# Gated recurrence of an RWKV-7 branch: the inverse's transposed copy made by 32x32 block transposes on VectorE

## The reference, cut to what matters

```python
def _rwkv7_step(S, inp):
    r, w, k, v, kk, a = inp
    sa = jnp.einsum('dbhij,dbhj->dbhi', S, -kk)
    S = S * w[..., None, :] + sa[..., None] * (kk * a)[..., None, :] + v[..., None] * k[..., None, :]
    y = jnp.einsum('dbhij,dbhj->dbhi', S, r)
    return S, y
```

## Time and profile before

| | us |
|---|---|
| median of 3 runs | 2967.43 (2967.22 to 2968.2) |
| span of the profiled execution | 2965.1 |
| TensorE busy in that span | 2912.8 (98%) |
| VectorE / ScalarE / GpSimd busy | 1483.8 / 1089.2 / 230.6 |
| share of the granted TensorE clock | 0.999 |

### The profile page before, as it was taken

How to read it: one execution, slowest core, us unless ns; L and a number is a source line. 1 busy time by engine, 2 the same in 40 slices (tenths; PEclk the granted TensorE clock), 3 DMA queues, 4 the chain that set the end, 5 groups by cost and what they waited for, 6 DMA issues and landing times.

```text
span 2965.1 us, 46938 instructions
## 1 busy us (share of the span) xinstructions
PE 2912.8 (98%) x21254; PEld 2417.4 (82%) x21254; DVE 1483.8 (50%) x1475; ACT 1089.2 (37%) x1180; POOL 230.6 (8%) x132
## 2 busy tenths in 40 slices
PE   9999999999999999999999999999999998999998
PEld 7788878888889888888888888878878887888886
DVE  6765554443454544443454444665577554544432
ACT  5554542222454732222342222542254422232222
POOL 1012110000100010000110000320002220000001
PEclk9999999999999999999999999999999999999999
DMA  4220022223322022223222223312220003222222
GB/s 146 79 68 2 30 86 97 89 99 114 106 88 86 29 86 99 100 89 117 100 94 92 98 101 110 110 66 84 102 93 5 4 5 117 100 100 96 90 102 82
DMA packets 44903, 249.31 MB, mean 84 GB/s; under 512 B 8443, under 2 KB 12283, under 8 KB 17184
## 3 DMA queue, kind: packets, MB, share of 16 engines
q1 hardware_dynamic: 43552, 242.11, 23.1%
q10 hardware_dynamic: 1152, 4.19, 0.3%
HBM read 237.90 MB, written 8.39 MB: 83 GB/s over the span
## 4 chain that ended last, share of the span: by engine, by line
PE 91%; DVE 5%; ACT 3%; issue 1%; DMA 0%; POOL 0%; SPq 0%; DVEq 0%; ACTq 0%
PE ps L666 72%; PE ps L2915 7%; PE ps L1521 2%; PE ps L2495 1%; PE ps L2205 1%; PE ps L3988 1%; PE ps L2479 1%; PE ps L3971 1%; PE ps L4000 1%; ACT whi L267 1%; PE ps L2176 0%; DVE wlo L273 0%; DVE gdn_conv L1146 0%; PE ps L3102 0%; PE ps L425 0%
## 5 line engine op out<-in xcount | busy, mean ns | idle before, releaser
L273 DVE TENSOR_TENSOR wlo<-wraw,whi 128x2048 fp32r<-128x2048 f32 x210 | 486.6, 2318 | 912.9 <-ACT whi L267 908.8
L267 ACT ACTIVATE whi<-wraw 128x2048 fp32r<-128x2048 f32 x210 | 402.1, 1915 | 900.1 <-PE ps L666 900.0
L666 PE MATMUL ps<-ffn_xh,whi 128*128 128x512 f32 x1408 | 549.2, 390 | 0.2 <-DVE wlo L273 0.2
L666 PE MATMUL ps<-ffn_xl,whi 128*128 128x512 f32 x1408 | 547.8, 389 | 0.0
L666 PE MATMUL ps<-ffn_xh,wlo 128*128 128x512 f32 x1408 | 547.8, 389 | 0.0
L666 PEld LDWEIGHTS ps<-ffn_xh,whi 128*128 128x128 f32 x1408 | 264.3, 188 | 57.3 <-DVE wlo L273 1.0
L666 PEld LDWEIGHTS ps<-ffn_xl,whi 128*128 128x128 f32 x1408 | 264.3, 188 | 55.2 <-issue 0.7
L666 PEld LDWEIGHTS ps<-ffn_xh,wlo 128*128 128x128 f32 x1408 | 264.3, 188 | 54.8
L666 PE MATMUL ps<-ffn_uh,whi 128*128 128x512 f32 x704 | 274.1, 389 | 0.0
L666 PE MATMUL ps<-ffn_uh,wlo 128*128 128x512 f32 x704 | 273.9, 389 | 0.0
L666 PE MATMUL ps<-ffn_ul,whi 128*128 128x512 f32 x704 | 273.9, 389 | 0.0
(11 more groups left out here) (525 smaller groups left out, 4685.7 us busy)
## 6 DMA issues: line engine op xcount, KB each, us to landing
wraw<-in_weights SPq DMA_DIRECT2D x211, 1024.0 KB, 4.8
gates_kept<-gates_tmp ACTq DMA_DIRECT2D x8, 512.0 KB, 4.1
mix_gate<-gates_kept SPq DMA_DIRECT2D x8, 512.0 KB, 11.1
h<-in_x SPq DMA_DIRECT2D x4, 512.0 KB, 8.5
mix_y<-hz_kept SPq DMA_DIRECT2D x2, 1024.0 KB, 6.2
out<-out SPq DMA_DIRECT2D x4, 512.0 KB, 3.1
wraw<-in_weights SPq DMA_DIRECT2D x2, 512.0 KB, 6.9
ple_raw<-in_p SPq DMA_DIRECT2D x4, 256.0 KB, 5.1
```

The costliest lines, as they stand in the source:

```text
L267: c.nc.scalar.activation(c.whi[:, j % 2, :], c.wraw[:, j % 2, :], ACT.Copy).then_inc(c.hi_ready, 1)
L273: c.nc.vector.tensor_tensor(c.wlo[:, j % 2, :], c.wraw[:, j % 2, :], c.whi[:, j % 2, :].bitcast(F32), ALU.subtract).then_inc(c.lo_ready, 1)
L666: last = nc.tensor.matmul(pair[:, m, :], a, b, start=opens and n == 0 and wa + xa == 0, stop=closes and n == len(ks) - 1 and wa == 1)
```

## The change

`pe_lower` and its semaphore place `LL` go, with VectorE's masked copy `offX` and its identity addition. In their place VectorE transposes XT into X in 32x32 blocks, right after XTi. At levels 0 to 3 no block is wider than 32, so the 32x32 block transpose of X is the transposed matrix: `pe_right` makes the new half of X alone (32 records in place of 64), VectorE adds it to X as before, waits for that addition and then transposes the whole X (128x512) into XT. At level 4, where blocks are 64 wide, `pe_right` makes XT's half as before. The left products of direction 1 get a PSUM bank of their own (the second F bank), and direction 1's new halves go to the first. The slots of all other work stay as they were.

```diff
@@ class Recurrence @@
-"kk", "lora", "vt", "BA", "LL", "KA", ...
+"kk", "lora", "vt", "BA", "KA", ...
-"off PT XTi", "offX MQ Xi", ...
+"off PT XTi Xi", "MQ", ...
+    def z_bank(self, l, d):
+        banks = self.F_BANK if d else self.Z_BANK
+        return banks[1] if l == LEVELS - 1 and d == 0 else banks[0]
+
+    def y_bank(self, d):
+        return self.F_BANK[1] if d else self.Y_BANK
@@ pe_build @@
         if s in (0, 2):
-            d = s // 2
-            self.pe_strict(pe, k, d)
-            if d == 0:
-                self.pe_lower(pe, k, 0)
+            self.pe_strict(pe, k, s // 2)
...
-        elif s == 4:
-            self.pe_lower(pe, k, 1)
@@ pe_left @@
-        out = self.bank(self.Y_BANK)
+        out = self.bank(self.y_bank(d))
         pe.wait_ge(*self.at("CT", 10 * k + 2 * l + d))
         if l:
             pe.wait_ge(*self.at("X", 8 * k + 2 * (l - 1) + d))
+            pe.wait_ge(*self.at("Yc", 10 * k + 2 * (l - 1) + d))
         else:
             pe.wait_ge(*self.at("Xi", 2 * k + d))
-        if l or d:
-            pe.wait_ge(*self.at("Yc", 10 * k + 2 * l + d - 1))
-        else:
-            pe.wait_ge(*self.at("offX", 2 * k + 1))
+            if d:
+                pe.wait_ge(*self.at("LT", 2 * k + 1))
+                pe.wait_ge(*self.at("PT", 2 * k + 1))
+            elif k:
+                pe.wait_ge(*self.at("Yc", 10 * k - 2))
@@ pe_right @@
-        if l < LEVELS - 1:
-            for n in range(NCH):
-                self.both(lambda r: self.columns(self.halved(banks[0])[r, n, :], l),
-                          lambda r: XT[r, d, n, :], lambda r: self.side(self.Y[r, d, n, :], l, d))
         for n in range(NCH):
-            last = self.both(lambda r: self.columns(self.halved(banks[1])[r, n, :], l), lambda r: self.Y[r, d, n, :],
-                             lambda r: self.side(XT[r, d, n, :], l, 1 - d))
+            if l < LEVELS - 1:
+                last = self.both(lambda r: self.columns(self.halved(bank)[r, n, :], l),
+                                 lambda r: XT[r, d, n, :], lambda r: self.side(self.Y[r, d, n, :], l, d))
+            else:
+                last = self.both(lambda r: self.columns(self.halved(bank)[r, n, :], l), lambda r: self.Y[r, d, n, :],
+                                 lambda r: self.side(XT[r, d, n, :], l, 1 - d))
@@ dve_build @@
             nc.vector.tensor_tensor(XT, XT, self.eyes(), ALU.add).then_inc(*self.done("XTi"))
+            dve.wait_ge(*self.at("XTi", 2 * k + d))
+            nc.vector.transpose(self.X[:, d, :, :], XT).then_inc(*self.done("Xi"))
         if s in (2, 5):
             d = s // 5
-            X = self.X[:, d, :, :]
-            dve.wait_ge(*self.at("LL", 2 * k + d))
-            nc.vector.tensor_tensor(X, self.bank(self.Y_BANK), self.masked(1 - d, 2), ALU.mult).then_inc(*self.done("offX"))
             dve.wait_ge(*self.at("KA", 2 * k + d))
             nc.vector.tensor_tensor(self.MQ[:, :, :], ...).then_inc(*self.done("MQ"))
-            dve.wait_ge(*self.at("offX", 2 * k + d))
-            nc.vector.tensor_tensor(X, X, self.eyes(), ALU.add).then_inc(*self.done("Xi"))
@@ dve_right @@
+        nc, XT = self.c.nc, self.XT[k % 2][:, d, :, :]
+        new = self.columns(self.c.ps[:, self.z_bank(l, d), 0:T // 2], l)
         dve.wait_ge(*self.at("Z", 10 * k + 2 * l + d))
         if l < LEVELS - 1:
             X = self.side(self.X[:, d, :, :].rearrange("p n t -> p (n t)"), l, d)
-            nc.vector.tensor_tensor(X, X, ...banks[0]..., ALU.add).then_inc(*self.done("X"))
-        XT = self.side(self.XT[k % 2][:, d, :, :].rearrange("p n t -> p (n t)"), l, 1 - d)
-        nc.vector.tensor_tensor(XT, XT, ...banks[1]..., ALU.add).then_inc(*self.done("XT"))
+            nc.vector.tensor_tensor(X, X, new, ALU.add).then_inc(*self.done("X"))
+            dve.wait_ge(*self.at("X", 8 * k + 2 * l + d))
+            nc.vector.transpose(XT, self.X[:, d, :, :]).then_inc(*self.done("XT"))
+        else:
+            two = self.side(XT.rearrange("p n t -> p (n t)"), l, 1 - d)
+            nc.vector.tensor_tensor(two, two, new, ALU.add).then_inc(*self.done("XT"))
```

More of the change, by code:

```diff
@@ L2753, in __init__ @@
         self.sems = {}
-        for engine, cycles in (("pe", ("kk", "lora", "vt", "BA", "LL", "KA", "MV", "Y", "Z", "tB tK", "z", "U", "dS",
+        for engine, cycles in (("pe", ("kk", "lora", "vt", "BA", "KA", "MV", "Y", "Z", "tB tK", "z", "U", "dS",
                                        "bonus turn g")),
@@ L2976, in pe_build @@
             self.pe_right(pe, k, 0, 0)
-        elif s < 26:
+        elif 10 <= s < 26:
             l, what = 1 + (s - 10) // 4, (s - 10) % 4
@@ L2981, in pe_build @@
             else:
-                self.pe_right(pe, k, l - 1 if what == 1 else l, what == 1)
+                self.pe_right(pe, k, l - 1 if what == 1 else l, int(what == 1))
         elif s == 26:
@@ L3000, in pe_strict @@
         last.then_inc(*self.done("BA"))
[L3002 to L3007, removed]
-        for n in range(NCH):
-            last = self.both(lambda r: out[r, n, :], lambda r: self.AR[k % 3][r, d, n, 0:C7], lambda r: self.B[b][r, d, n, :])
-        last.then_inc(*self.done("LL"))
     def pe_keys(self, pe, k, d):
@@ L3049, in pe_right @@
     def pe_right(self, pe, k, l, d):
-        banks, XT = (self.F_BANK if d else self.Z_BANK), self.XT[k % 2]
-        d = int(d)
+        bank, XT = self.z_bank(l, d), self.XT[k % 2]
         pe.wait_ge(*self.at("Yc", 10 * k + 2 * l + d))
@@ L3196, in act_left @@
             act.wait_ge(*self.at("Z", 10 * k + 2 * (l - 1) + d))
-        self.c.nc.scalar.activation(self.Y[:, d, :, :], self.bank(self.Y_BANK), ACT.Copy).then_inc(*self.done("Yc"))
+        self.c.nc.scalar.activation(self.Y[:, d, :, :], self.bank(self.y_bank(d)), ACT.Copy).then_inc(*self.done("Yc"))
     def act_prepare(self, act, p, s):
@@ L3370, in dve_right @@
     def dve_right(self, dve, k, l, d):
-        nc, banks = self.c.nc, (self.F_BANK if d else self.Z_BANK)
+        nc, XT = self.c.nc, self.XT[k % 2][:, d, :, :]
+        new = self.columns(self.c.ps[:, self.z_bank(l, d), 0:T // 2], l)
         dve.wait_ge(*self.at("Z", 10 * k + 2 * l + d))
@@ L3374, in dve_right @@
             X = self.side(self.X[:, d, :, :].rearrange("p n t -> p (n t)"), l, d)
-            nc.vector.tensor_tensor(X, X, self.columns(self.c.ps[:, banks[0], 0:T // 2], l), ALU.add).then_inc(*self.done("X"))
-        XT = self.side(self.XT[k % 2][:, d, :, :].rearrange("p n t -> p (n t)"), l, 1 - d)
-        nc.vector.tensor_tensor(XT, XT, self.columns(self.c.ps[:, banks[1], 0:T // 2], l), ALU.add).then_inc(*self.done("XT"))
+            nc.vector.tensor_tensor(X, X, new, ALU.add).then_inc(*self.done("X"))
[4 more added lines that the diff above has]
+            nc.vector.tensor_tensor(two, two, new, ALU.add).then_inc(*self.done("XT"))
     def dve_prepare(self, dve, p, s):
```

## The result

The changed kernel takes 2951.36 us (median; 2950.62 to 2951.99) against 2967.32: a ratio of 0.9946, 95% interval 0.9932 to 0.9960, 16.0 us faster. The forecast was 2944, 23.5 us faster. The direction and the range held; the size is two thirds of the forecast, and what is missing was lost in one place, period k = 0.

What follows compares the result with a forecast made beforehand. TensorE was taken as the bound, k = 0 nearly even with VectorE. 36.8 + 1.8 + 0.7 - 8.4 - 2.7 - 2.75 - 0.4 - 1.5 = 23.5 us gained, forecast 2944 us, range 2927 to 2958.

Steps and rivals of the forecast that it cites:

- TensorE's products, 36.8 us: TensorE, building periods: 32 right-product halves and 8 lower products removed, 40 x 0.92 = 36.8 us gained.
- The transpose, 0.68 us: VectorE: each 128x512 transpose taken as 0.68 us, starts 0.60 apart, range 0.42 to 2.32.
- The bank of direction 1, 1.8 us: Left products of direction 1 no longer share a PSUM bank; TensorE's waits for ScalarE's Y copy fall away, 1.8 us gained.
- k = 1 to 3, 21.9 us: Building periods k = 1 to 3: the gain of 23.5 us less the 1.6 of k = 0.
- The new waits of 5.45 us: TensorE in k = 1 and 2 waits longer for Zs, ST and vt's copy: 2.7 and 2.75 us lost.
- ysum's copy where 1.5 was said: Openings of k = 1 to 3: second key product waits for ScalarE's copies MVc and ysc, 1.5 us lost.
- k = 0, 1.6 us gained: Period k = 0: VectorE sets the pace from slot 9 to 24; last transpose product of keys ends 1.6 us earlier, 8.4 lost.
- I carried the starts forward: k = 0: VectorE's starts recomputed with 0.60 us per 128x512 operation and 0.54 us more per right product.
- TensorE alone: Rival: TensorE alone decides, the new waits are hidden; 38.6 us gained, 2929 us, chance 0.18.
- GpSimd holding the transposes: Rival: level transposes held by GpSimd's masks, 1.07 us each, 22 on the path; no change, 2967; no-change chance 0.06.
- A transpose of 1.2 us or more: Rival: transposes of about 1.2 us make VectorE the bound in k = 0 to 2; 11 us less gain, 2955, chance 0.13.
- transposes that cost more than the products: Rival: blocks of 4-byte elements need several passes; at 2.32 us each, 25 us slower, 2993; chance of slower 0.07.

Runs made afterwards that it cites:

- the filler: The changed kernel plus 32 TensorE records with unused results behind each right product of levels 0 to 3 in k = 0: 2941.14 us, ratio 0.9914.

## Why the prediction was right, and where it was wrong

**TensorE's products, 36.8 us.** The count (1280 records) and the price (0.92 us for 32 at full clock) were right: the halves left still take 1.07 us each as durations where the clock is 1.00.

**The transpose, 0.68 us.** Measured 0.711, with 0.63 between starts. The wait of 0.20 us behind X came out shorter: X starts at 2233.57, the transpose at 2234.02, 0.45 us for X of 0.41, where the sum had 0.62.

**The bank of direction 1, 1.8 us.** The waits for ScalarE's Y copy are gone from the changed kernel's list of waits.

**k = 1 to 3, 21.9 us.** Measured 23.8, or 25.1 with k = 2 as it is without its stretch at half clock (64.61). The new waits of 5.45 us (2.7 + 2.75) in k = 1 and 2 were too high: k = 1 gained 8.1 where 6.6 was said (68.1 to 61.5). TensorE's waits for VectorE and ScalarE, kernel after, 2266 to 2456 us:

```profile
PE ps L2922 <- DVE rw_Zs L3309: 2.6, 4, 0.9
PE ps L3110 <- ACT rw_vt L3232: 1.6, 1, 1.6
PE ps L2922 <- DVE rw_ST L3316: 1.2, 2, 0.9
PE ps L2922 <- ACT rw_ysum L3171: 0.8, 3, 0.3
```

Before, the same list had 1.1, 0.5 and 0.7 us for Zs, ST and vt's copy, 2.3 together; here they are 2.6 + 1.2 + 1.6 = 5.4. That is 3.1 us of new waits, and 0.8 for ysum's copy where 1.5 was said. The kinds of wait were right, vt's 0.7 to 1.6 among them; the sum is a little over half of the 5.45.

**k = 0, 1.6 us gained.** This is the step that failed. "I carried the starts forward" took every product at its full-clock price. The chain it found is real: with the clock held, k = 0 takes 56.70 us where it said 56.25. What it left out is that TensorE's waits in this period could cost it its clock. They did, and the products between the waits then took 1.7 us between starts in place of 0.92. That turned 1.15 us of gain into 6.9 of loss: 8.05 us, shown by the filler.

That the forecast still came within a third of its size is partly luck: k = 0 was 8.5 us worse than said, and k = 1 to 3, where the new waits were priced too high, gave 1.9 us back. With the clock held in k = 0 the kernel takes 2941.14, 25.5 us under the kernel before beside it (2966.67), against the 23.5 that the forecast said: the sum without the clock was near, and a little low.

**The rivals.** TensorE alone (2929): out; k = 0 is VectorE's. GpSimd holding the transposes: none of the 40 was held (711 to 712 ns). Only 5 of them overlap a mask, by 0.41 us at most, so they mostly missed each other as the forecast argued; where they meet, as in the run with later transposes, they aren't held either. But GpSimd holds others (t, av, B or K, up to 1.75 us in place of 0.69), and without its masks in k = 0 the loss is gone. *A transpose of 1.2 us or more* and *transposes that cost more than the products* (2955, 2993): out, by 0.711.

## What to carry to other kernels

When a change takes work off a TensorE that is nearly always busy, ask in each stage where it will wait afterwards, and price a stage of frequent waits at half clock as well as at full: in k = 0 the two differ by 8 us. These runs give no rule for which of the two prices holds: k = 1 waited too and kept its clock. A period in which the other engine is nearly even is not "no gain" but a possible loss. Where a run shows that the clock fell, a few products that nobody reads, placed where TensorE waits anyway, got it back; where it hadn't fallen they cost 3.3 us. And a fall of the clock in one kernel can hang on a third engine: here on GpSimd's masks, which make VectorE's operations long. Read the granted clock by stage: the mean over the span said 0.993 and hid a stage at 0.76.

## What the runs showed of the hardware

TensorE's granted clock went to 0.50 (1.2 GHz) in k = 0 behind a window in which it was busy for 2.58 of 4.00 us; with filler the same window had 3.57 of 4.00 and the clock stayed at 1.00. The busy time alone doesn't tell the cases apart: with GpSimd's masks cut TensorE was busy 2.06 of 4.00 us from 2247.5 on, and the clock stayed at 1.00. At half clock 32 records took 1.80 to 1.97 us in place of 1.07 to 1.15. While GpSimd multiplied two SBUF tensors, VectorE operations with two SBUF inputs took up to 1.76 us in place of 0.69. A 32x32 block transpose of 128x512 (one input) never took more than 0.712, also where it ran beside GpSimd for its whole length.
